# Two halves of an activation chunk as one 512-column operand: the merge and branch stage of a two-layer float32 kernel

## The reference, cut to what matters

```python
g = jax.nn.sigmoid(h @ w_merge + b_merge)          # (256, 2048) @ (2048, 4096)
g_a, g_p = jnp.split(g, N_BRANCHES, axis=-1)
merged = g_a * (y_a @ w_br_attn) + g_p * (y_p @ w_br_pool)   # each (256, 1024) @ (1024, 2048)
o = merged @ w_out                                 # (256, 2048) @ (2048, 2048)
return x + gate[:, None] * rmsnorm_2(o, post_g)
```

## Time and profile before

| | |
|---|---|
| median of 3 runs | 1749.76 us (1748.15 to 1753.54) |
| span of the profiled execution (first to last instruction) | 1745.0 us |
| time of the median run outside such a span | 4.8 us |
| PE busy | 1718.9 us, 99% |
| DVE busy | 1041.1 us, 60% |
| ACT busy | 834.4 us, 48% |
| GpSimd (POOL) busy | 25.2 us, 1% |
| mean granted TensorE clock | 0.996 of full |

### The profile page before, as it was taken

One profiled execution on the slowest core, in us unless ns is written; L12 is line 12 of the kernel. 1 busy time (PEld: TensorE's weight loads), 2 busy tenths in 40 slices (PEclk: granted clock), 3 DMA queues, 4 the chain that ended last, 5 costly groups with the idle time before them and its releaser, 6 DMA issues.

```text
span 1745.0 us, 28992 instructions
## 1 busy us (share of the span) xinstructions
PE 1718.9 (99%) x11037; PEld 1544.7 (89%) x11037; DVE 1041.1 (60%) x1079; ACT 834.4 (48%) x1080; POOL 25.2 (1%) x39
## 2 busy tenths in 40 slices
PE   9999999999999999999999999999999999999997
PEld 6888888789988899889987998799799999999986
DVE  4544536456667677767776667775545545545554
ACT  6446564454444444444454445454434444444442
POOL 1000000010000000000000000000000000000000
PEclk9999999999999999999999999999999999999998
DMA  8542554566777677777776777765545655555562
GB/s 307 181 145 80 179 151 150 157 211 236 265 255 265 230 256 260 266 253 255 250 259 240 266 253 265 229 231 168 169 145 173 189 183 185 184 183 185 174 206 73
DMA packets 170791, 362.71 MB, mean 208 GB/s; under 512 B 10892, under 2 KB 15308, under 8 KB 170433
## 3 DMA queue, kind: packets, MB, share of 16 engines
q1 hardware_dynamic: 168416, 352.63, 61.3%
q0 software_dynamic: 2272, 8.60, 1.4%
HBM read 359.03 MB, written 2.15 MB: 207 GB/s over the span
## 4 chain that ended last, share of the span: by engine, by line
PE 57%; issue 26%; DVE 1%; DVEq 0%; ACT 0%; POOL 0%; POOLq 0%; ACTq 0%
PE G L609 29%; PE G L592 25%; PE S L579 1%; PE G L598 1%; PE S L899 0%; PE S L912 0%; DVE o_sb L1536 0%; PE S L869 0%; PE S L880 0%; PE S L884 0%; PE G L747 0%; DVE x_nf L1441 0%; PE S L892 0%; PE S L860 0%; ACT tmp_T L1000 0%
## 5 line engine op out<-in xcount | busy, mean ns | idle before, releaser
L1196 DVE TENSOR_TENSOR w_lo<-raw,w_hi 128x1024 fp32r<-128x1024 f32 (+2 forms) x576 | 690.1, 1208 | 537.1 <-ACT w_hi L950 534.7
L950 ACT ACTIVATE w_hi<-raw 128x1024 fp32r<-128x1024 f32 (+2 forms) x576 | 596.2, 1046 | 600.3 <-PE G L592 327.7
L592 PE MATMUL G<-Y_hi,w_hi 128*128 128x256 f32 x1952 | 548.5, 281 | 7.1 <-issue 6.2
L592 PE MATMUL G<-Y_hi,w_lo 128*128 128x256 f32 x1952 | 545.9, 280 | 0.0
L592 PE MATMUL G<-Y_lo,w_hi 128*128 128x256 f32 x1952 | 545.4, 279 | 0.0
L609 PE MATMUL G<-w_hi,X_hi 128*128 128x512 f32 (+2 forms) x992 | 384.3, 387 | 1.5 <-DVE w_lo L1196 1.0
L609 PE MATMUL G<-w_hi,X_lo 128*128 128x512 f32 (+2 forms) x992 | 379.8, 383 | 0.0
L609 PE MATMUL G<-w_lo,X_hi 128*128 128x512 f32 (+2 forms) x992 | 379.5, 383 | 0.0
L592 PEld LDWEIGHTS G<-Y_hi,w_hi 128*128 128x128 f32 x1952 | 367.6, 188 | 10.2 <-issue 8.9
L592 PEld LDWEIGHTS G<-Y_lo,w_hi 128*128 128x128 f32 x1952 | 367.7, 188 | 0.4 <-issue 0.2
L592 PEld LDWEIGHTS G<-Y_hi,w_lo 128*128 128x128 f32 x1952 | 367.6, 188 | 0.0
(11 more groups left out here) (268 smaller groups left out, 1137.1 us busy)
## 6 DMA issues: line engine op xcount, KB each, us to landing
raw<-in_w_in SPq DMA_DIRECT2D x144, 512.0 KB, 4.4
raw<-in_w_mlp_in SPq DMA_DIRECT2D x128, 512.0 KB, 6.0
raw<-in_w_mlp_out SPq DMA_DIRECT2D x128, 512.0 KB, 6.6
ada_w<-in_w_ada SPq DMA_DIRECT2D x64, 768.0 KB, 4.4
raw<-in_w_out SPq DMA_DIRECT2D x64, 512.0 KB, 4.5
raw<-in_w_merge SPq DMA_DIRECT2D x64, 512.0 KB, 4.3
raw<-in_w_branch_attn SPq DMA_DIRECT2D x16, 512.0 KB, 4.4
raw<-in_w_branch_pool SPq DMA_DIRECT2D x16, 512.0 KB, 5.3
```

Source lines behind the costliest of these rows:

```text
L592: ins = nc.tensor.matmul(G[:, bank, j // 2, TOK * (j % 2):TOK * (j % 2 + 1)], w[:, s % SPLIT, c, cut], a[:, c0 + c, :], start=first and c ...
L950: nc.scalar.activation(w_hi[:, s % SPLIT, :, 0:n], raw[:, k, :, 0:n], ACT.Copy).then_inc(hi_ready, 1)
L1196: nc.vector.tensor_tensor(w_lo[:, s % SPLIT, :, 0:n], raw[:, k, :, 0:n], w_hi[:, s % SPLIT, :, 0:n], ALU.subtract).then_inc(lo_ready, 1)
```

## The change

Four things change together.

1. `X` and `Y` are stored as pairs: for each chunk of 128 features, 256 columns of high halves and behind them 256 columns of low halves.
2. P4 uses a new `gemm_pair`. For each chunk and each of four feature groups, one matmul with `w_hi` stationary moves the whole 512-column pair into a whole PSUM bank, and one with `w_lo` stationary moves the 256 high columns into the bank's first half. A bank then holds (high part) and (low part) of 256 tokens beside each other, which have to be added when it is read. A block takes four banks: the attention side uses the four of S, the pooling side the four of G.
3. VectorE does that addition, as a reduction over the two halves (`add_halves`), in `gate_a`, `gate_p`, `br_a` and `br_p`. The sigmoid now reads and writes SBUF.
4. The addition of the two branch products and the low half `M_lo` move from DVE to POOL.

P5's blocks take the banks in the order S, S, G, G.

```diff
+O_BANK = [2, 3, 0, 1]
...
-        fifth += block("w_out_2", n * NW, NW, ALL, "M", n % 2)
+        fifth += block("w_out_2", n * NW, NW, ALL, "M", O_BANK[n])
...
-stage("P4", 7, "gate_a", A=1)
-stage("P4", 15, "gate_p", A=1)
-stage("P4", 19, "br_a", D=1)
-stage("P4", 23, "br_p", A=1, D=3)
+stage("P4", 7, "gate_a", A=1, D=1)
+stage("P4", 15, "gate_p", A=1, D=1)
+stage("P4", 19, "br_a", D=2)
+stage("P4", 23, "br_p", A=1, D=2, G=2)
...
-        x_hi, at = put("X_hi", at, [P, KC, TOK], f32r)
-        x_lo, at = put("X_lo", at, [P, KC, TOK], f32r)
+        x_pair, at = put("X_pair", at, [P, KC, 2, TOK], f32r)
+        x_hi, x_lo = x_pair[:, :, 0, :], x_pair[:, :, 1, :]
...
+            def gemm_pair(s, loop, slot, lhs, c0, banks, first, last):
+
+                pe.wait_ge(lo_ready, count(s, loop, 1))
+                both = PAIR[lhs]
+                for c in range(SUB):
+                    for j, bank in enumerate(banks):
+                        cut = slice(P * j, P * (j + 1))
+                        nc.tensor.matmul(bank, w_hi[:, s % SPLIT, c, cut],
+                                         both[:, c0 + c, :, :].rearrange("p a q -> p (a q)"),
+                                         start=first and c == 0, stop=False, skip_group_check=True)
+                        ins = nc.tensor.matmul(bank[:, 0:TOK], w_lo[:, s % SPLIT, c, cut], both[:, c0 + c, 0, :],
+                                               start=False, stop=last and c == SUB - 1, skip_group_check=True)
                 ins.then_inc(used, 1)
...
-                    gemm(s, loop, slot, (lhs, c0 + SUB * p, b, NW, p == 0, p == last), 4)
+                    gemm_pair(s, loop, slot, lhs, c0 + SUB * p, (S_BANKS, G_BANKS)[b], p == 0, p == last)
...
                 elif name in ("gate_a", "gate_p"):
                     k = 0 if name == "gate_a" else 1
-                    act.wait_ge(used, count(PHASE["P4"][0], (i, MERGE_SUBS), 8 * (k + 1)))
+                    act.wait_ge(dve_side, done("D", name, i))
                     for c in range(4):
-                        ins = nc.scalar.activation(sig[:, k, c, :], G[:, k, c // 2, TOK * (c % 2):TOK * (c % 2 + 1)], ACT.Sigmoid,
+                        ins = nc.scalar.activation(sig[:, k, c, :], sig[:, k, c, :], ACT.Sigmoid,
                                                    bias=vecs[:, bass.ds(i * 4 + V_MER + KC * k + c, 1)])
                     ins.then_inc(act_side, 1)
                 elif name == "br_p":
-                    act.wait_ge(dve_side, step("D", name, 2, i))
+                    act.wait_ge(pool_side, step("G", name, 1, i))
                     nc.scalar.activation(m_hi[:, bass.ds(i * 4, 4), :], sig[:, 0, :, :], ACT.Copy).then_inc(act_side, 1)
...
+            def add_halves(dst, four):
+
+                banks = four[:, :, :].rearrange("p b (h q) -> p b q h", h=2) if four is S else \
+                    four[:, :, :, :].rearrange("p a b (h q) -> p (a b) q h", h=2)
+                return nc.vector.tensor_reduce(dst, banks, axis=AX.X, op=ALU.add)
...
+                elif name in ("gate_a", "gate_p"):
+                    k = 0 if name == "gate_a" else 1
+                    dve.wait_ge(used, count(PHASE["P4"][0], (i, MERGE_SUBS), 8 * (k + 1)))
+                    add_halves(sig[:, k, :, :], (S, G)[k]).then_inc(dve_side, 1)
+                elif name in ("br_a", "br_p"):
+                    k = 0 if name == "br_a" else 1
+                    dve.wait_ge(used, count(PHASE["P4"][0], (i, MERGE_SUBS), 20 + 4 * k))
+                    add_halves(br[:, :, :], (S, G)[k]).then_inc(dve_side, 1)
                     dve.wait_ge(dve_side, step("D", name, 1, i))
-                    nc.vector.tensor_tensor(sig[:, 0, :, :], sig[:, 0, :, :], sig[:, 1, :, :], ALU.add).then_inc(dve_side, 1)
-                    dve.wait_ge(act_side, done("A", name, i))
-                    nc.vector.tensor_tensor(m_lo[:, bass.ds(i * 4, 4), :], sig[:, 0, :, :], m_hi[:, bass.ds(i * 4, 4), :],
-                                            ALU.subtract).then_inc(dve_side, 1)
+                    nc.vector.tensor_tensor(sig[:, k, :, :], br[:, :, :], sig[:, k, :, :], ALU.mult).then_inc(dve_side, 1)
...
+            with pool.Fori(0, QUARTERS) as i:
+                enter(pool, "br_p", i)
+                pool.wait_ge(dve_side, done("D", "br_p", i))
+                nc.gpsimd.tensor_tensor(sig[:, 0, :, :], sig[:, 0, :, :], sig[:, 1, :, :], ALU.add).then_inc(pool_side, 1)
+                pool.wait_ge(act_side, done("A", "br_p", i))
+                nc.gpsimd.tensor_tensor(m_lo[:, bass.ds(i * 4, 4), :], sig[:, 0, :, :], m_hi[:, bass.ds(i * 4, 4), :],
+                                        ALU.subtract).then_inc(pool_side, 1)
```

More of the change, by code:

```diff
@@ L358, in program @@
         Y_AT = (room - 64 - 32 * KB) // 32 * 32
-        y_hi, _ = put("Y_hi", Y_AT, [P, KC, TOK], f32r)
-        y_lo, _ = put("Y_lo", Y_AT + 16 * KB, [P, KC, TOK], f32r)
+        y_pair, _ = put("Y_pair", Y_AT, [P, KC, 2, TOK], f32r)
+        y_hi, y_lo = y_pair[:, :, 0, :], y_pair[:, :, 1, :]
         swa, at = put("swa", AR, [P, NT, SWA_END])
@@ L422, in program @@
         pool_m, at = put("pool_m", at, [P, NT, 4, TOK])
-        sig, _ = put("sig", AR, [P, 2, 4, TOK])
+        sig, at = put("sig", AR, [P, 2, 4, TOK])
+        br, _ = put("br", at, [P, 4, TOK])
         m_hi, at = put("M_hi", AR + 16 * KB, [P, KC, TOK], f32r)
@@ L436, in program, with token_bank @@
         OPER = {"X": (x_hi, x_lo), "Y": (y_hi, y_lo), "M": (m_hi, m_lo)}
+        PAIR = {"X": x_pair, "Y": y_pair}
+        def token_bank(bank, tt):
+            return G[:, bank, tt, :] if bank < 2 else S[:, 2 * (bank - 2) + tt, :]
+        S_BANKS = [S[:, k, :] for k in range(4)]
+        G_BANKS = [G[:, k // 2, k % 2, :] for k in range(4)]
         raw_in = [sem(f"raw_in{k}") for k in range(RAW)]
@@ L641, in _ @@
                 need("P3", k, "D", step("D", "h2_T0", 4 + 2 * k + 2) if k < 4 else done("D", f"h2_T{k - 3}"))
[L642 to L647, removed]
+            need("P5", 0, "G", done("G", "br_p", QUARTERS - 2))
+            need("P5", 0, "D", step("D", "br_a", 1, QUARTERS - 1))
+            need("P5", 6, "G", done("G", "br_p", QUARTERS - 1))
             def loop_waits(phase, s, i):
@@ L665, in loop_waits @@
                 else:
-                    after7, after8 = (done("A", "yp1") - done("A", n) for n in ("inb7", "inb8"))
                     if s == 0:
-                        pe.wait_ge(dve_side, i * TURN["P4"]["D"] + step("D", "gate_a", 0) - 3)
-                        pe.wait_ge(act_side, i * TURN["P4"]["A"] + step("A", "gate_a", 0) - after7)
+                        pe.wait_ge(dve_side, i * TURN["P4"]["D"] + step("D", "br_a", 1) - TURN["P4"]["D"])
                     if s == 8:
-                        pe.wait_ge(dve_side, i * TURN["P4"]["D"] + step("D", "gate_a", 0) - 2)
-                        pe.wait_ge(act_side, i * TURN["P4"]["A"] + step("A", "gate_a", 0) - after8)
+                        pe.wait_ge(dve_side, i * TURN["P4"]["D"] + step("D", "br_p", 1) - TURN["P4"]["D"])
+                        pe.wait_ge(act_side, i * TURN["P4"]["A"] + step("A", "gate_a", 0) - (done("A", "yp1") - done("A", "inb8")))
                     if s == 16:
-                        pe.wait_ge(act_side, done("A", "gate_a", i))
-                        pe.wait_ge(dve_side, step("D", "br_a", 0, i))
+                        pe.wait_ge(dve_side, done("D", "gate_a", i))
                     if s == 20:
-                        pe.wait_ge(act_side, done("A", "gate_p", i))
+                        pe.wait_ge(dve_side, done("D", "gate_p", i))
             def main(s, loop, slot, phase=None, i=None, local=None):
@@ L1528, in stages @@
                             rms_sum()
[L1529 removed]
+                        ins = nc.vector.tensor_tensor(o_sb[:, tt, c], token_bank(O_BANK[n], tt), row[:, c], ALU.mult)
                     ins.then_inc(dve_side, 1)
```

14 lines of the change are left out of this document (3 added, 11 removed).

## The result

The changed kernel takes **1758.01 us** in the median (4 runs, 1757.23 to 1759.33), the kernel before 1748.95 us beside it: a ratio of 1.0052, 95% interval 1.004 to 1.0063. It is slower by half a per cent. The prediction said 1754.7, with a range of 1746 to 1764.

The account below looks back on a forecast made before the run. PE was taken as the bound, P4 lasting as long as its matmuls' start-to-start distances. Terms -6.3 (wide matmul) + 9.6 (chain behind `br_p`) + 1.6 (clock) = +4.9 us on 1749.8 gave 1754.7 us, range 1746 to 1764.

Parts of the forecast that it names:

- Part 1: P4's matmuls: merging pairs of 256 columns into one of 512 saves 6.3 us, ends 4.6 and 8.0.
- Part 2: New PSUM banks and paired layout: earlier gate starts bring nothing, and the other stages' moved addresses cost nothing.
- Part 3: `add_halves` on VectorE takes 2.27 us each, upper end 4.4; at the gates it fits with 0.6 us to spare.
- Part 4: At P4's turn ends, reduction and POOL's addition delay `w_lo`, so PE stands: +9.6 us together, 4.7 to 11.6.
- X: Time of POOL's addition of the branch products behind `br_p`: taken as 2.2 us, between 0.96 and 2.7.
- 8.83 - 1.3 + 2.2 - 8.16 = 1.6: PE's wait for `w_lo` in P5 behind P4's last turn, where no table load stands: 1.6 us.
- Hidden: POOL's `M_lo` ends near 9.6 us into the turn, P5 needs it at 16 us: no cost.
- Part 5: PE's stalls in P4 bring one spell at the 1.2 GHz level: +1.6 us, ends 0 and 4.7.
- POOL quick: Rival: POOL's addition takes 0.96 to 1.3 us, stalls too short for the clock, 1748 to 1750 us; chance 0.15.
- The narrow matmul cheap: Rival: a wide matmul ahead hides the 256-column matmul's weight load, 8.4 us more saved, 1746.3 us; chance 0.10.
- Merging worth next to nothing: Rival: a wide matmul always costs 233.2 ns, so merging saves only 1.8 us, 1759.2 us; chance 0.10.
- The slow PSUM read: Rival: strided reductions take 4.4 us, delaying gates and the chain behind `br_p`, 1769 us; chance 0.12.

Follow-up runs that it names:

- experiment 2: The changed kernel with `M_hi` on POOL as well, so that ScalarE waits for nothing at `br_p`: 1743.03 us against 1749.47 for the kernel before, ratio 0.9961.
- experiment 3: The kernel before with only the paired layout of `X` and `Y`: 1749.59 us against 1749.47, ratio 1.0.
- Experiment 5: The changed kernel with POOL's `M_lo` held back until DVE has made the splits PE wants next: 1756.71 us against 1748.64 for the kernel before, ratio 1.0046.
- Experiment 4: The kernel before with only the addition and `M_lo` moved to POOL, three attempts: 1755.99 (faulty wait), 1753.46 (new tile moved `M`), 1751.54 us against 1749.82.
- Experiment 6: The changed kernel with filler matmuls ahead of sub 3 of each P4 turn: six 1767.05 us against 1748.64, three 1758.04 against 1749.82 (kernel before).
- experiment 1: The changed kernel with the addition and `M_lo` back on VectorE: 1748.44 us against 1749.47 for the kernel before, ratio 0.9989.
- experiment 7: The kernel before with `Y` at a multiple of 64 bytes: 1763.48 us against 1748.64; with the split weights moved by 32 bytes: 1782.42 against 1749.82.

## Why the prediction was right, step by step

- **Part 1, the wide matmul: right.** Four `X` subs took 1441.91 - 1430.82 = 11.09 us, 2.772 each (predicted 2.774), the eight `Y` subs between the two gate reductions (1397.50 to 1419.72) 22.21 us, 2.776 each (2.782). That is 64 x 0.050 + 32 x 0.110 = 6.7 us, and P4 of experiment 2 shows 6.8 (predicted 6.3). The price of the pair was right and its parts were not: with `X` 230.0 + 116.7 ns in place of 226.7 + 120, the same sum, which is luck. The formula that the prediction quotes from the Trainium skill, TensorE: Matmul & The Clock Gate, section "Back-to-back issue gap", would have left 1.9 us of it. That page of the Trainium skill gives the formula for an isolated matmul, and for a stream of weight loads and matmuls about 131 ns at 512 columns. The runs agree with neither.
- **Part 2, banks and layout at nothing: right** (experiment 3).
- **Part 3, the reduction 2.27 us: right,** 2.29 us, out of S as out of G; the strided PSUM read costs nothing of its own, and no gap stood behind a gate.
- **Part 4, the chain behind `br_p`: the mechanism right, the size too small.** Predicted 9.6 us, measured 3 x 2.89 + 3.02 = 11.7. X was 2.40 us, not 2.2; that is 0.2 in each of three turns. The estimate of 2.25 us, half of what the Trainium skill, GPSIMD Engine Reference, section "Elementwise — side-by-side cycle accounting", gives for 2048 elements, was nearer. The term that failed is the one behind the last turn, "8.83 - 1.3 + 2.2 - 8.16 = 1.6": it takes 1.23 us for `w_lo` where 2.68 were measured, because `M_lo` on POOL ran beside it. Experiment 5 takes that away and leaves 1.78 - 0.23 = 1.55 us. Experiment 4 had it without the reduction: 2.70 us for `w_lo` beside `M_lo`. I had put `M_lo` down as "Hidden" by asking when its result is needed, and not whom it runs beside. (Its end was put at 9.6 us into the turn, where the terms add up to 9.5; it came at 10.1.) By the Trainium skill, SBUF — State Buffer, section "Who interferes with whom", a DVE instruction with two SBUF inputs contends with a GpSimd instruction that reads SBUF; the traces here agree, with 2.68 us for 1.22 and, in experiment 2, up to 3.43.
- **Part 5, the clock: right in kind, one spell too few.** One was counted at 1.6 us, and two came, at 1.6 each; that there would be one was a choice between none and three, and no row gave it. Experiment 6 shows that the spells between turns go when the gaps are filled: none in six filled gaps, five in six unfilled ones of the changed kernel and experiment 5. Which gap is followed by one is not settled: two of three here, all three in experiment 5, none behind experiment 1's gaps of 1.76 us, and behind P5's gap of 3.2 us one in experiment 6 and none in the changed kernel.
- **The sum.** -6.7 + 11.7 + 3.2 = +8.2 us, against 9.1 between the medians (7 to 11 by the interval) and 10.4 between the two profiled spans, of which 1.3 are P2's scatter. The prediction's +4.9 lacked 2.1 in part 4 and 1.6 in part 5, and had 0.4 too little in part 1. So it found 4.9 of 9.1 us: the chain and its place were foreseen, the size only roughly, and it gave a measurable slowdown no more than a chance of 0.51. The 4.8 us that it put outside the span are less: executions with both figures lie 1.8 to 2.2 us over their span, and the rest is the profiled execution, faster than the median. The forecast added both to its difference and does not change by it.
- **The rivals.** POOL quick: no, 2.40 us. The narrow matmul cheap: no, it stayed at 116.7 to 118.3 ns. Merging worth next to nothing: no. The slow PSUM read: no.

## What to carry to other kernels

When work is moved to a slower engine, look at who waits for its result: an engine that issues in written order passes such a wait on to all that stands behind it. Move the whole chain, so that the feeding engine waits for nothing, and the slow engine costs nothing here (1743.0 us). Leave one link where the feeding engine must wait, and two edits that gain 1.0 and cost 1.7 us alone cost nine together: both draw on the same 0.9 us of lead, and the gaps grow long enough to bring slow clock and a collision with them. Price also whom the moved instruction runs beside, and, in an experiment, what a new tile does to the addresses of those behind it.

## What the runs showed of the hardware

- In a run of matmuls of one width, each with its weight load, the pace depends on the operands' offsets modulo 64 bytes: alike, 120.0 ns (256 columns) and 226.7 ns (512); 32 bytes apart, 117 to 118 and 233.3 ns. Moving the weights by 32 bytes cost this kernel 33 us of 1750 (experiment 7).
- DVE's `w_lo`, with two inputs in SBUF, and a POOL instruction that reads SBUF take turns, nearly as if the one that began later stood until the other was through. Begun second, `w_lo` ended 1.08 to 1.09 us behind POOL's end every time, whether it then took 2.68 us (`M_lo` unchanged, 2.37), 3.43, or 2.05 beside the one-input copy of experiment 2. Begun second, POOL's addition took 3.32 us in place of 2.40, the first 1.04 to 1.06 of it beside a `w_lo` that took its usual 1.22.
- A matmul of 512 columns on plain float32 operands took 5.2 / 6 = 0.86 us, nearly four times one on rounded operands (experiment 6).
- DVE reduced 2048 elements of PSUM, halves 1 KB apart, in 2.29 us, where a reduction of 1024 elements side by side in SBUF took 1.22.
